# DeltaNet chunk inverse in f32: each level multiplies the inverse and its transpose separately, 64 columns at a time, with the masking on VectorE

## The reference

```python
decay = where(incl, exp(g[..., :, None] - g[..., None, :]), 0)
a = where(strict, einsum('bhnid,bhnjd->bhnij', k * beta, k) * decay, 0)
t_inv = triangular_solve(eye + a, eye)            # inverse of (1 + a)
u = t_inv @ (v * beta)
w = t_inv @ (k * beta * exp(g))
# scan over chunks, state s per head
v_new = u - w @ s
o = (q * exp(g)) @ s + attn @ v_new
s = s * g_last + k_dec.T @ v_new
```

## Time and profile before

| | us |
|---|---|
| median of 3 runs | 2888.64 |
| lowest and highest | 2885.36 to 2889.18 |
| the profiled execution | 2863.73 |
| its span, first to last instruction | 2861.9 |
| mean granted TensorE clock | 0.969 |
| TensorE busy | 2579.1 |
| VectorE busy | 1749.0 |
| ScalarE busy | 1554.9 |
| Pool busy | 763.2 |

### The profile page before, as it was taken

How to read it: one execution, slowest core, us unless ns; L and a number is a source line. 1 busy time by engine, 2 the same in 40 slices (tenths; PEclk the granted TensorE clock), 3 DMA queues, 4 the chain that set the end, 5 groups by cost and what they waited for, 6 DMA issues and landing times. The chain is left out here.

```text
span 2861.9 us, 132892 instructions
## 1 busy us (share of the span) xinstructions
PE 2579.1 (90%) x55873; PEld 2233.2 (78%) x55873; DVE 1749.0 (61%) x1936; ACT 1554.9 (54%) x1833; POOL 763.2 (27%) x586
## 2 busy tenths in 40 slices
PE   8999997899898886699999999998988999999993
PEld 2444556788788744598998998988888999999993
DVE  2334894544544477617254648577787767878883
ACT  3522543433433543527364647677777767767883
POOL 1201003453543211212222222232222322233331
PEclk9999998999999998699999999999999999999997
DMA  9500001000000221917456659688998887979975
GB/s 364 198 30 32 1 1 37 19 24 16 18 26 15 85 91 74 372 31 273 131 198 207 216 189 329 229 322 320 336 368 308 302 284 277 326 281 344 357 279 195
DMA packets 124476, 536.74 MB, mean 188 GB/s; under 512 B 12540, under 2 KB 13552, under 8 KB 91616
## 3 DMA queue, kind: packets, MB, share of 16 engines
q1 hardware_dynamic: 107120, 481.80, 44.8%
q0 software_dynamic: 14464, 47.79, 7.4%
q10 hardware_dynamic: 2832, 6.37, 0.6%
HBM read 496.99 MB, written 38.92 MB: 187 GB/s over the span
## 5 line engine op out<-in xcount | busy, mean ns | idle before, releaser
L2200 PE MATMUL ps<-qkv,weights 128*128 128x64 f16 x10496 | 936.6, 193 | 59.9 <-DVE weights L1696 24.4
L2200 PEld LDWEIGHTS ps<-qkv,weights 128*128 128x128 f16 x10496 | 921.6, 98 | 73.9 <-issue 36.0
L2201 PE MATMUL ps<-qkv,weights 128*128 128x64 f16 x10496 | 936.2, 193 | 2.3 <-issue 2.3
L2202 PE MATMUL ps<-qkv,weights 128*128 128x64 f16 x10496 | 936.2, 193 | 0.0
L2201 PEld LDWEIGHTS ps<-qkv,weights 128*128 128x128 f16 x10496 | 922.0, 98 | 2.4 <-issue 2.4
L2202 PEld LDWEIGHTS ps<-qkv,weights 128*128 128x128 f16 x10496 | 922.0, 98 | 0.0
L1696 DVE SCALAR_TENSOR_TENSOR weights<-hT,weights 128x2048 f16<-128x2048 f16 (+1 forms) x256 | 585.8, 2343 | 158.3 <-ACT weights L1160 129.4
L1160 ACT ACTIVATE weights<-hT 128x2048 f16 (+1 forms) x256 | 527.2, 2102 | 74.1 <-DMA hT<-in_w_gu_dram 57.6
L2217 PE MATMUL ps<-qkv,weights 128*128 128x64 f16 x5248 | 472.3, 193 | 24.5 <-DVE weights L1701 22.2
L2217 PEld LDWEIGHTS ps<-qkv,weights 128*128 128x128 f16 x5248 | 461.3, 98 | 32.2 <-DVE weights L1701 27.7
L2218 PE MATMUL ps<-qkv,weights 128*128 128x64 f16 x5248 | 472.0, 193 | 0.0
(11 more groups left out here) (395 smaller groups left out, 3971.8 us busy)
## 6 DMA issues: line engine op xcount, KB each, us to landing
hT<-in_w_gu_dram SPq DMA_DIRECT2D x256, 1024.0 KB, 8.8
qkv<-in_w_down_dram SPq DMA_DIRECT2D x128, 1024.0 KB, 6.1
weights<-in_w_ada_dram SPq DMA_DIRECT2D x12, 2048.0 KB, 15.7
qkv<-in_w_in_dram SPq DMA_DIRECT2D x4, 2048.0 KB, 7.8
hT<-decay_rows SPq DMA_DIRECT2D x20, 256.0 KB, 3.4
hT<-beta_rows SPq DMA_DIRECT2D x20, 256.0 KB, 4.0
qkv<-in_x_dram ACTq DMA_DIRECT2D x8, 512.0 KB, 6.8
weights<-in_w_in_dram SPq DMA_DIRECT2D x2, 2048.0 KB, 14.3
```

Source lines behind the costliest of these rows:

```text
L2200: pe.matmul(dst, ghi[k][:, b, c], xT[:, 0, k, :], start=first, stop=False, skip_group_check=True)
L2201: pe.matmul(dst, ghi[k][:, b, c], xT[:, 1, k, :], start=False, stop=False, skip_group_check=True)
L2202: last = pe.matmul(dst, glo[k][:, b, c], xT[:, 0, k, :], start=False, stop=end, skip_group_check=True)
```

## The change

The inverse is no longer turned by transposes at every level. Both `t` and `tT` are kept up by a product of their own, and each of the three products of a level moves only half of the columns, the ones in which that level changes something: `half_of` picks every second block of 2^l columns, and `half_bank` is a PSUM bank's first half. The matrix `aT` is used unmasked as the stationary operand; the mask is applied by VectorE to the first product on its way into `prod`, which is cleared once before the loop. The columns of `prod` outside the half hold what earlier levels left; the rows of the transpose's product that stem from them are multiplied by the zeros of a column of zeros and ones (`idx_f`) when VectorE adds it to `tT`. The inverse's own product VectorE adds to `t`. ScalarE copies nothing in levels 1 to 6, and Pool masks only level 0. The scaled add of the key-state products is split: direction 0 behind level 2, direction 1 behind level 3. The DMA of the beta rows and the staging on Pool wait for other events, since `aT` and the keys are now read at other times. One transpose, at level 0, is left.

```diff
--- before.py
+++ after.py
@@ -180,7 +180,7 @@
         mhalf = sb("mhalf", [P, 8])
         gng = sb("gng", [P, P])
         idx_i = sb("idx_i", [P, 8], I32)
-        idx_f = sb("idx_f", [P, 8])
+        idx_f = sb("idx_f", [P, 16])
 
 
         def carve(region, sizes):
@@ -361,7 +361,7 @@
         e_Q = Event(sem("qk_and_transposes_done"), 2)
         e_KV = Event(sem("values_ready"), 2)
         e_KA = Event(sem("decayed_keys_ready"), 2)
-        e_B = Event(sem("level_blocks_ready"), 2 * LEVELS)
+        e_B = Event(sem("first_level_blocks_ready"), 2)
         e_qd = Event(sem("decayed_queries_ready"), 2)
         NL = LEVELS - 1
         e_P = Event(sem("level_first_product_done"), 2 * NL)
@@ -472,6 +472,12 @@
         def bank(r, i):
             return ps[:, 4 * r + i, :].rearrange("p (h q) -> p h q", h=H)
 
+        def half_bank(r, i, l):
+            return ps[:, 4 * r + i, 0:H * P // 2].rearrange("p (h g w) -> p h g w", h=H, w=1 << l)
+
+        def half_of(a, l, i):
+            return a.rearrange("p h (g two w) -> p h g two w", two=2, w=1 << l)[:, :, :, i, :]
+
         block = es.enter_context(nc.Block())
 
         def rowvec(ap, n=P):
@@ -548,7 +554,7 @@
                     sp.sem_inc(s_idle, 1)
                     sp.dma_start(dn[r]["eg"], g_d[r, bass.ds(n * DIRS * H + r * H, H), :].rearrange("h q -> (h q)").partition_broadcast(P)
                                  ).then_inc(s_w[2 * r], 16)
-                    e_B.before(sp, s, 2 * NL + r)
+                    e_P.before(sp, s, 2 * (NL - 1) + r)
                     sp.sem_inc(s_idle, 1)
                     sp.dma_start(dn[r]["aT"], b_d[bass.ds(n * DIRS * H + r * H, H), :].rearrange("h q -> (h q)")
                                  .partition_broadcast(P)).then_inc(s_w[2 * r + 1], 16)
@@ -744,6 +750,8 @@
                     e_Q.before(pool, s, r)
                     e_KV.before(pool, s, r)
                     pool.sem_inc(s_idle, 1)
+                    e_ws.before(pool, s, r)
+                    pool.sem_inc(s_idle, 1)
                     e_qd.before(pool, s, r)
                     pool.sem_inc(s_idle, 1)
                     pool.tensor_copy(gst[:, r, :], gdec[:, bass.ds(n, 1), 4 * r:4 * r + 4].rearrange("p a h -> p (a h)"))
@@ -752,31 +760,22 @@
                     if out:
                         pool.tensor_copy(d["qc"], qkvT[:, 0:H, bass.ds(n * P, P)])
                     pool.tensor_copy(d["vc"], qkvT[:, 2 * H:3 * H, bass.ds(n * P, P)]).then_inc(e_st.sem, 1)
-                for l in range(LEVELS):
-                    for r in range(DIRS):
-                        d = dn[r]
-                        if l == 0:
-                            e_A.now(pool, s, r)
-                            pool.sem_inc(s_idle, 1)
-                        if l >= 3:
-                            e_P.now(pool, s, 2 * (l - 3) + r)
-                            pool.sem_inc(s_idle, 1)
-                        elif l >= 1:
-                            e_P.before(pool, s, 2 * (l + LEVELS - 4) + r)
-                            pool.sem_inc(s_idle, 1)
-                        mask = neg0 if l == 0 else same[:, l - 1, :]
-                        dst = d["u"] if l == 0 else d["b%d" % (l % 2)]
-                        m = mask[:] if l == 0 else mask
-                        pool.tensor_tensor(dst, d["aT"], m.unsqueeze(1).to_broadcast([P, H, P]),
-                                           ALU.mult).then_inc(e_B.sem, 1)
-                        if l == 1 and out:
-                            e_D.now(pool, s, r)
-                            pool.sem_inc(s_idle, 1)
-                            e_o.before(pool, s, r)
-                            pool.sem_inc(s_idle, 1)
-                            pool.tensor_tensor(d["qd"], d["qc"], d["eg"], ALU.mult).then_inc(e_qd.sem, 1)
-                        elif l == 1:
-                            pool.sem_inc(e_qd.sem, 1)
+                for r in range(DIRS):
+                    d = dn[r]
+                    e_A.now(pool, s, r)
+                    pool.sem_inc(s_idle, 1)
+                    pool.tensor_tensor(d["u"], d["aT"], neg0[:].unsqueeze(1).to_broadcast([P, H, P]),
+                                       ALU.mult).then_inc(e_B.sem, 1)
+                for r in range(DIRS):
+                    d = dn[r]
+                    if out:
+                        e_D.now(pool, s, r)
+                        pool.sem_inc(s_idle, 1)
+                        e_o.before(pool, s, r)
+                        pool.sem_inc(s_idle, 1)
+                        pool.tensor_tensor(d["qd"], d["qc"], d["eg"], ALU.mult).then_inc(e_qd.sem, 1)
+                    else:
+                        pool.sem_inc(e_qd.sem, 1)
 
             deltanet(pool, turn)
 
@@ -1028,7 +1027,7 @@
                     act.activation(square[:, j % 2, 0:n], qkvT[:, ct, t0:t0 + n], ACT.Square).then_inc(s_sq, 1)
 
 
-            for e in (e_D, e_KA, e_Pc, e_Xc, e_vn):
+            for e in (e_D, e_KA, e_Xc, e_vn):
                 e.ahead(act)
 
             def turn(s, out):
@@ -1040,23 +1039,14 @@
                         act.activation(d["eg"], d["eg"], ACT.Exp)
                     act.activation(ge[:, r, :], gs[:, r, :], ACT.Exp)
                     act.activation(d["decay"], d["decay"], ACT.Exp).then_inc(e_D.sem, 1)
-                for l in range(LEVELS):
-                    for r in range(DIRS):
-                        d = dn[r]
-                        if l >= 1:
-                            e_P.now(act, s, 2 * (l - 1) + r)
-                            act.activation(d["prod"], bank(r, 0), ACT.Copy).then_inc(e_Pc.sem, 1)
-                    for r in range(DIRS):
-                        d = dn[r]
-                        if l == 0:
-
-                            e_Q.now(act, s, r)
-                            for h in range(H):
-                                last = act.activation(d["kdec"][:, h, :], bank(r, 0)[:, h, :], ACT.Copy, scale=ge[:, r, 8 + h:9 + h])
-                            last.then_inc(e_KA.sem, 1)
-                        if l < NL:
-                            e_X.now(act, s, 2 * l + r)
-                            act.activation(d["t"], bank(r, 2), ACT.Copy).then_inc(e_Xc.sem, 1)
+                for r in range(DIRS):
+                    d = dn[r]
+                    e_Q.now(act, s, r)
+                    for h in range(H):
+                        last = act.activation(d["kdec"][:, h, :], bank(r, 0)[:, h, :], ACT.Copy, scale=ge[:, r, 8 + h:9 + h])
+                    last.then_inc(e_KA.sem, 1)
+                    e_X.now(act, s, r)
+                    act.activation(d["t"], bank(r, 2), ACT.Copy).then_inc(e_Xc.sem, 1)
                 for r in range(DIRS):
                     d = dn[r]
                     e_u.now(act, s, r)
@@ -1315,6 +1305,9 @@
             for l in range(1, LEVELS - 1):
                 link(dve.tensor_tensor(same[:, l - 1, :], same[:, l - 1, :], same[:, l, :], ALU.subtract))
             link(dve.tensor_tensor(same[:, LEVELS - 2, :], same[:, LEVELS - 2, :], ones[:], ALU.subtract))
+            link(dve.tensor_single_scalar(idx_i[:, 1:7], idx_i[:, 1:7], 1, ALU.bitwise_and))
+            link(dve.tensor_copy(idx_f[:, 9:15], idx_i[:, 1:7]))
+            link(dve.tensor_scalar(idx_f[:, 1:7], idx_f[:, 9:15], -1.0, 1.0, ALU.mult, ALU.add))
 
             def low_w(w):
 
@@ -1447,7 +1440,8 @@
             dve.sem_inc(s_zero, 1)
             for r in range(DIRS):
                 link(dve.memset(dn[r]["state"], 0.0))
-            for e in (e_E, e_A, e_T, e_R, e_S):
+                link(dve.memset(dn[r]["prod"], 0.0))
+            for e in (e_E, e_A, e_T, e_Pc, e_R, e_S):
                 e.ahead(dve)
 
 
@@ -1489,17 +1483,29 @@
                     dve.tensor_tensor(d["vb"], bank(r, 1), spread(bst[:, r, :]), ALU.mult).then_inc(e_KV.sem, 1)
                 for l in range(1, LEVELS):
                     for r in range(DIRS):
+                        e_P.now(dve, s, 2 * (l - 1) + r)
+                        mask = same[:, l - 1, :].rearrange("p (g two w) -> p g two w", two=2, w=1 << l)[:, :, r, :]
+                        dve.tensor_tensor(half_of(dn[r]["prod"], l, r), half_bank(r, 0, l),
+                                          mask.unsqueeze(1).to_broadcast([P, H, P >> (l + 1), 1 << l]),
+                                          ALU.mult).then_inc(e_Pc.sem, 1)
+                    for r in range(DIRS):
                         d = dn[r]
+                        if l < NL:
+                            t = half_of(d["t"], l, r)
+                            e_X.now(dve, s, 2 * l + r)
+                            dve.tensor_tensor(t, t, half_bank(r, 2, l), ALU.add).then_inc(e_Xc.sem, 1)
+                        tT = half_of(d["tT"], l, 1 - r)
                         e_TP.now(dve, s, 2 * (l - 1) + r)
-                        dve.tensor_tensor(d["tT"], d["tT"], bank(r, 1), ALU.add).then_inc(e_T.sem, 1)
-                    if l == 2:
-                        for r in range(DIRS):
-                            d = dn[r]
```

(33 more changed lines are left out.)

## The result

The changed kernel is slower: 2979.17 us, median of four runs (2978.83 to 2995.11), against 2888.31 for the kernel before; the ratio is 1.033 [1.0295, 1.0365]. The forecast was 3004 in a range of 2897 to 3122. The profiled execution took 2978.83 us, its span is 2977.1 and its mean granted clock 0.943, where it was 0.969 before.

What follows compares the result with a forecast made beforehand. The prediction took the dependency chain to bound the old levels and TensorE's issue the new. Ten turns at +11.6 us, +116, less 0.8 for small parts, gave +115 on the median 2888.64: 3004 us, range 2897 to 3122.

Steps and rivals of the forecast that it cites:

- The load pace: TensorE in the levels: the weight load sets the pace, 0.1116 us an instruction at full clock, whatever the columns.
- Rival C: Levels: a 64-column product costs half, 0.056 us; turn 12.3 us shorter, kernel 2766 us; chance 0.07 with weaker forms.
- The bound moves from the chain to TensorE's issue: Levels at full clock: 48 TensorE instructions take 5.36 us a level, replacing the dependency chain's 5.13 us.
- The full-clock sum for a turn: One latent turn without a clock drop: preparation 13.20, levels 32.7 and last products 7.14 us.
- The wait of level 4: TensorE waits 0.5 us for level 4's mask, queued on VectorE behind direction 1's four key-state operations.
- The clock: Narrow levels hold a full clock but don't raise a low one; the preparation's drop lasts until the key-state products.
- A2: Clock falls again at level 4's wait, low through level 6: +22.4 us a turn, 3112 us; chance 0.31 with all-low case.
- Rival B: Clock as before, one drop of 3.4 us a turn: +2.2 us a turn, 2910 us; chance 0.23.
- A: Main case: clock low through levels 1 and 2, levels 43.8 us against 32.22, kernel 3004 us; chance 0.35.
- +116 for ten: DeltaNet loop: the loss of 11.6 us a latent turn, applied to all ten turns.
- Smaller parts: Around the levels: shorter context-turn adds -2.1 us, two memsets +1.3; masks off Pool, beta DMA and Pool's staging nothing.

Runs made afterwards that it cites:

- after_filled: The changed kernel with 24 more 128-column instructions a turn in the waits around level 0's transposes, results overwritten: 2889.46 us, ratio 1.0026.
- wide: The changed kernel with every product of levels 1 to 6 moving all 128 columns again, VectorE still treating halves: 2901.39 us, ratio 1.0058.
- level1_wide: The changed kernel with 128 moving columns in level 1 only: 2903.43 us, ratio 1.0059.
- ws_early: The changed kernel with the 128-column key-state products issued behind level 1's first products instead of behind level 2: 2917.35 us, ratio 1.0122.
- turned_narrow: `turned_wide` with the first product and the transpose's product moving 64 columns, transposes still wide: 2901.31 us, ratio 1.0056.
- turned_wide: `wide` without the inverse's own product and its add, with transposes and ScalarE's half copies in their place: 2867.44 us, ratio 0.9932.
- before_half_reads: The kernel before with only ScalarE's copy of t and VectorE's add to tT treating the changed half: 2868.00 us, ratio 0.9948.

## Why the prediction was right, and where its size was off

**The load pace.** Right. The forecast took 0.1116 us an instruction whatever the columns, from a 4-column pair and a 128-column group. Measured in between: 0.1116 at 64 columns, and a level of 5.36 us at 64 and at 128. Rival C, a gain from half the columns, is out. The Trainium skill gives an issue gap of some 60 cycles for up to 64 columns ("TensorE: Matmul & The Clock Gate", section "Back-to-back issue gap"), but for a product by itself: the section says that at few columns this counts too little, since the weight load is missing from it. The rows here agree with that remark, and the forecast's reading of the figure as rival C passed over it.

**The bound moves from the chain to TensorE's issue.** Right. In the levels at full clock TensorE is busy 19.27 of 19.50 us, and level 5 is 48 x 0.1116. The mask took 0.42 as estimated. The full-clock sum for a turn was 13.20 + 32.7 + 7.14 = 53.0 us; `after_filled` shows 53.15.

**The wait of level 4.** Right in place and size, 0.44 us against 0.5 (changed kernel, level 4):

```profile
853.11 1.12 DVE L1506 SCALAR_TENSOR_TENSOR hT<-ps,bg,hT 128x128 f32<-128x128 f32 x4
854.15 0.77 DVE L1488 TENSOR_TENSOR weights<-ps,same 128x256 f32<-128x256 f32 x2
```

The four operations of direction 1 stand ahead of the mask, which starts at 854.15, and TensorE goes on at 854.68 in place of 854.24.

**The clock.** Right in mechanism and close in each level: 43.98 us against 43.8, levels 1 and 2 at 10.09 and 10.24 against 10.25, the key-state products with level 3's first ones at 5.35 against 3.0 + 1.8, the full clock from there on. A2 wanted the clock to fall again at level 4's wait: it didn't, in this turn or in the others. Rival B wanted only the short drop. Which of the three would come was a judgement from two stretches of f16 products, with a chance of 0.35 for A against 0.31 and 0.23, so that A came true is in part luck; `wide`, `level1_wide` and `ws_early` show its mechanism.

The Trainium skill (same page, "Why this matters for your kernels") wants TensorE kept busy without a break to get and to hold the full clock. Here it was busy 23.50 of 23.50 us and stayed at 0.50, so under these light products the rule didn't bring the clock back. It also warns of idle gaps between bursts of products; but no wait in this latent turn's preparation is longer than 1.46 us, shorter than those it warns of, and the clock fell all the same. The measurement decides here.

**What was mis-sized: "+116 for ten".** The latent turns rose by 11.65 us on average, from (974.00 - 554.73) / 8 = 52.41 to (1068.00 - 555.56) / 8 = 64.06; forecast 11.6. But there are eight of them. The two context turns take 52.42 and 48.37 us, and before they took 52.77 and 48.05 (they begin at 453.91 and 506.68 and end at 554.73). Eight turns at 11.6 make 93 us and not 116; 23 of the 25 us between 3004 and 2979 are this term. The forecast had priced all ten turns from a latent one. Two windows of the kernel before, in its second context turn, show that this was another case:

```profile
513.00:514.00 1.00, 1.00 (x8) 0.87 (x6) 0.96 (x2) 0.55 (x3) 1.00 (x1) 0.62 0.00 0
...
519.00:520.00 1.00, 1.00 (x7) 1.00 (x6) 0.07 (x1) 0.64 (x2) 1.00 (x2) 0.50 0.00 0
```

The drop began some 5 us ahead of level 1 (which started at 518.70) and reached just into it. In the changed kernel it was over before level 1; in `turned_narrow` it began within level 1 and cost this turn 7.3 us. The windows of before would not have told which way that falls, but they would have told to price these two turns by themselves, at anything from nothing to 11.6 each. The timed execution at 2995.11 may be one in which they were hit; no trace shows it.

**Smaller parts.** The loop starts 0.87 us later, in line with the two memsets (+1.3). The shorter adds of the context turns are there: in the second one the two adds of the identity take 2.35 us together, against 3.41 before, 1.06 less as forecast. The time from the row of transposes at 513.25 to level 1 is 518.12 - 513.25 = 4.87 us against 518.70 - 512.74 = 5.96, though under clocks that weren't the same. But the rest of that turn, with more instructions, is 37.44 us against 36.03, so that the two turns together come out within 0.1 us of before. Preparation as a whole is 13.08 against 13.20, so the later DMA of the beta rows and the other wait of Pool's staging cost nothing, as argued.

**The whole loss, split.** From `wide` to the changed kernel, 78 us: the low clock that the narrow columns prolong. From `wide` to `turned_wide`, 34 us: the own product. 0.55 in each of five levels of ten turns is 27.5, and the wait of level 4 goes with it: that level falls from 865.59 - 859.74 = 5.85 us in `wide` to 833.80 - 829.00 = 4.80. Against these stands what the change brings where it isn't bound by TensorE: masks and adds on halves and products with the unmasked `aT`. `turned_wide`, which keeps these, is 19 us faster than the kernel before; `before_half_reads` shows that the half-width add and copy alone bring 14. About 15 us more (2867.44 to 2852.19) are the drops that `turned_wide` still has, one of some 6.8 us in four of its eight latent turns; the kernel before has such drops too, shorter and in most turns.

What the chip counts when it takes or gives back the clock stays open; the runs only show what it did.

## What to carry to other kernels

Count the f32 products, not their columns: a product costs two weight loads whether it moves 4, 64 or 128 columns, so cutting the moving side buys nothing, and a product in place of a transpose doubles the instructions of that step. When the operations become lighter, look at what runs right behind each drop of the granted clock, because here light work stretched a drop of 3.4 us to more than 20. Waits that can't be avoided can be filled with wide work that nobody reads, if it ends before what is waited for. And a per-turn price is multiplied only by the turns in which its cause occurs.

## What was not expected of the hardware

Adding work made the kernel faster: 24 instructions a turn, 240 in all, took the changed kernel from 2979 to 2889 us and `turned_wide` from 2867 to 2852, at no cost in the turn that had no drop (49.87 and 49.88 us). VectorE reading every second block of 2^l columns in PSUM took no longer than reading contiguous ones: the add of 256 elements takes 0.42 us strided in `before_half_reads` and contiguous in the changed kernel. And the products of 32 columns didn't only fail to bring the clock back, they lost it again in the middle of uninterrupted work: TensorE was busy without a pause from 722 to 758, and the clock fell from 1.00 to 0.50 at about 725.
